# Stick-breaking prompt attention: the sums of the later key blocks are built up on VectorE instead of in TensorE's accumulation

## What is computed

```python
def sb_weights(z, valid):
    log_stay = jnp.where(valid, jax.nn.log_sigmoid(-z), 0.0)
    log_after = lax.cumsum(log_stay, axis=z.ndim - 1, reverse=True) - log_stay
    return jnp.where(valid, jnp.exp(jax.nn.log_sigmoid(z) + log_after), 0.0)

def sb_attend(qb, qpos, k, v, kpos, bias):
    z = sb_logits(qb, k, bias)
    a = sb_weights(z, kpos[None, :] < qpos[:, None])
    return jnp.einsum('bhqk,bkhd->bqhd', a.astype(v.dtype), v)
```

## Time and profile before

| what | value |
|---|---|
| median of three runs | 1826.12 us (1821.38 to 1830.33) |
| the profiled execution | 1838.87 us, its span 1837.0 us |
| TensorE busy | 1698.0 us, 92% of the span |
| VectorE busy | 701.4 us, 38% |
| ScalarE busy | 441.0 us, 24% |
| GpSimd busy | 186.4 us, 10% |
| mean granted TensorE clock | 0.936 of full speed |

### The profile page before, as it was taken

The page is one execution under the profiler, slowest core; times in us unless marked ns, Lnnn a source line. Parts: engine busy times, 40 slices in busy tenths (PEclk is TensorE's granted clock), DMA queues, the critical chain, the costliest instruction groups (busy, mean ns, idle before and its releaser), DMA issues.

```text
span 1837.0 us, 27196 instructions
## 1 busy us (share of the span) xinstructions
PE 1698.0 (92%) x10382; PEld 1443.8 (79%) x10382; DVE 701.4 (38%) x2932; ACT 441.0 (24%) x648; POOL 186.4 (10%) x271
## 2 busy tenths in 40 slices
PE   6997978879999779999899799999998999999997
PEld 4886856657777368998797577777887999999996
DVE  2048547656888435344502200000234323332223
ACT  2001145422232422222301220000124222222112
POOL 1000001100000055355103100000000000000000
PEclk9998988979999789999769899999988999999998
DMA  3269644447887100000054778773421323332231
GB/s 96 69 228 315 226 176 133 128 161 270 275 285 273 38 1 1 1 1 1 13 172 138 229 240 275 239 261 119 117 59 57 92 82 91 93 90 77 85 94 47
DMA packets 222895, 245.73 MB, mean 134 GB/s; under 512 B 8985, under 2 KB 184211, under 8 KB 222723
## 3 DMA queue, kind: packets, MB, share of 16 engines
q1 hardware_dynamic: 222766, 244.00, 41.6%
HBM read 232.56 MB, written 11.60 MB: 133 GB/s over the span
## 4 chain that ended last, share of the span: by engine, by line
PE 83%; DVE 6%; DMA 4%; ACT 3%; POOL 2%; issue 1%; SPq 1%; POOLq 0%; DVEq 0%; ACTq 0%
PE ps L713 32%; PE ps L731 24%; PE ps L757 3%; PE ps L808 3%; PE ps L955 3%; DMA kring<-in_cache_k 2%; PE ps L966 2%; PE ps L821 2%; PE ps L970 2%; PE ps L698 1%; PE ps L1041 1%; DVE kring L1469 1%; PE ps L855 1%; PE ps L781 1%; POOL kring L1977 1%
## 5 line engine op out<-in xcount | busy, mean ns | idle before, releaser
L713 PE MATMUL ps<-xn,wring 128*128 128x268 f32 (+1 forms) x2336 | 544.5, 394 | 7.0 <-DVE xn L1452 4.4
L713 PEld LDWEIGHTS ps<-xn,wring 128*128 128x128 f32 (+1 forms) x2336 | 442.2, 191 | 116.4 <-issue 29.4
L1469 DVE CUSTOM_DVE_ANT_0 kring<-kring,qv 128x128 f32<-128x128 f32 x1024 | 225.0, 289 | 74.3 <-DMA kring<-in_cache_k 74.1
L1168 ACT ACTIVATE R<-ps 128x536 f32<-128x536 f32 x86 | 53.0, 616 | 511.7 <-PE ps L713 349.8
L426 DVE TENSOR_TENSOR wring_split<-wring,vring_split 128x1024 fp32r<-128x1024 f32 (+1 forms) x76 | 90.8, 1195 | 212.0 <-ACT vring_split L419 212.0
L731 PE MATMUL ps<-xn_split,vring_split 128*128 128x268 f32 x704 | 146.3, 289 | 8.0 <-DVE obT_split L440 8.0
L731 PE MATMUL ps<-obT_split,vring_split 128*128 128x268 f32 x704 | 145.1, 288 | 0.0
L731 PE MATMUL ps<-xn_split,wring_split 128*128 128x268 f32 x704 | 144.7, 287 | 0.0
L419 ACT ACTIVATE vring_split<-wring 128x1024 fp32r<-128x1024 f32 (+1 forms) x76 | 78.5, 1034 | 178.7 <-DMA wring<-in_w_ffn_out 106.8
L731 PEld LDWEIGHTS ps<-xn_split,vring_split 128*128 128x128 f32 x704 | 110.6, 190 | 8.8 <-issue 7.8
L731 PE MATMUL ps<-R_split,vring_split 128*128 128x268 f32 x592 | 114.1, 290 | 2.3 <-DVE rows_split L440 2.3
(11 more groups left out here) (333 smaller groups left out, 2159.6 us busy)
## 6 DMA issues: line engine op xcount, KB each, us to landing
kring<-in_cache_k SPq DMA_DIRECT2D x128, 512.0 KB, 5.0
vring<-in_cache_v SPq DMA_DIRECT2D x76, 512.0 KB, 5.4
wring<-in_w_in SPq DMA_DIRECT2D x72, 512.0 KB, 4.6
kring<-in_cache_v SPq DMA_DIRECT2D x52, 512.0 KB, 4.9
wring<-in_w_ffn_in SPq DMA_DIRECT2D x44, 512.0 KB, 3.8
wring<-in_w_ffn_out SPq DMA_DIRECT2D x16, 512.0 KB, 3.7
qv<-qdram SPq DMA_DIRECT2D x8, 512.0 KB, 6.1
out_rec_sample<-R SPq DMA_DIRECT2D x4, 1024.0 KB, 9.1
```

Of the source, the lines that this page charges most:

```text
L713: last = mm(ps[0:m, 2 * (t % 2) + i, 0:HALF], w_block(p, kk), src[:, k, i * HALF:i * HALF + HALF], start=(k == 0), stop=(k == n_k - 1))
L1168: go(halves(dst), pair(t, m), func).then_inc(act_read, 1)
L1469: m = v.tensor_tensor_reduce(kh, kh, qbc[:, b % 2, h * P:h * P + P], 1.0, 0.0, ALU.mult, ALU.add, dz[:, b % 4, p * H + h:p * H + h + 1])
```

## The change

One more triangle, tri_lt (ones where the key is above the diagonal, the complement of tri_ge), is made with the constants. VectorE gets a function suffixes: after GpSimd has masked sps of a head, it adds the rows of block kt + 1 to those of block kt, from the last block to the first, so that block kt then holds, partition by partition, its own softplus values and those of all later blocks. The five additions of a head wait for each other by a semaphore, s_suf. TensorE's later_sums then takes at most two matmuls per piece: tri_ge times block kt, and tri_lt times block kt + 1 (since tri_ge + tri_lt is the matrix of ones, this is the same sum). TensorE waits for s_suf in place of s_msp.

```diff
-CONSTS = 11
+CONSTS = 12
...
+SUFFIX = [(3, 512, LP), (2, 384, LP), (1, 256, LP), (0, 128, 512), (0, 512, LP)]
+
...
                 def later_sums(h):
-                    pe.wait_ge(s_msp, h + 1)
+                    pe.wait_ge(s_suf, len(SUFFIX) * (h + 1))
                     if h >= 1:
                         pe.wait_ge(s_arg, h)
                     for kt, a, b, bank, col in SB_PIECES:
-                        parts = [(tri_ge, kt, a)] + [(ones, k2, max(a, P * k2)) for k2 in range(kt + 1, TT)
-                                                     if P * k2 < b]
+                        parts = [(tri_ge, kt, a)]
+                        if kt + 1 < TT and P * (kt + 1) < b:
+                            parts.append((tri_lt, kt + 1, max(a, P * (kt + 1))))
...
+                def suffixes(h):
+
+                    dve.wait_ge(s_msp, h + 1)
+                    for i, (kt, a, b) in enumerate(SUFFIX):
+                        f, f2 = sb_at(kt, a)[2], sb_at(kt + 1, a)[2]
+                        if i:
+                            dve.wait_ge(s_suf, len(SUFFIX) * h + i)
+                        v.tensor_tensor(sps[:, h % 2, f:f + b - a], sps[:, h % 2, f:f + b - a],
+                                        sps[:, h % 2, f2:f2 + b - a], ALU.add).then_inc(s_suf, 1)
+
                 for h in (0, 1):
                     magnitude(h)
                     softplus(h)
+                suffixes(0)
+                suffixes(1)
                 for h in range(H):
                     dve.wait_ge(s_c, h + 1)
...
                     if h + 2 < H:
                         softplus(h + 2)
+                        suffixes(h + 2)
...
-            for m in (ones, tri_ge, tri_le, tri_gt):
+            for m in (ones, tri_ge, tri_le, tri_gt, tri_lt):
...
+            keep(tri_lt[:, :], tri_lt[:, :], [[1, P]], 0, -1, ALU.is_gt).then_inc(const_ready, 1)
```

More of the change, by code:

```diff
@@ L230, in build @@
         tri_gt = sb("tri_gt", [P, P])
+        tri_lt = sb("tri_lt", [P, P])
         lvl, lvl2 = twins("lvl", [P, 7, P])
@@ L373, in build @@
         s_s, s_z, s_abs, s_exp, s_ln, s_sp = (sem(n) for n in ("s_s", "s_z", "s_abs", "s_exp", "s_ln", "s_sp"))
+        s_suf = sem("s_suf")
         s_msp, s_c, s_arg, s_marg, s_w, s_av, s_o = (sem(n) for n in ("s_msp", "s_c", "s_arg", "s_marg", "s_w", "s_av", "s_o"))
@@ L1886, in _ @@
             g_.memset(selv[:, :], 0.0).then_inc(const_step, 1)
-            pool.wait_ge(const_step, 7)
+            pool.wait_ge(const_step, 8)
             keep(ident[:, :], ident[:, :], [[-1, P]], 0, 1, ALU.not_equal, 1.0).then_inc(const_ready, 1)
@@ L1898, in _ @@
                 keep(v[:, :, 0, :], v[:, :, 0, :], [[-2 * s, nb], [0, s]], -s, 1).then_inc(const_step, 1)
-            pool.wait_ge(const_step, 7 + 14)
+            pool.wait_ge(const_step, 8 + 14)
             for i in range(7):
```

## The result

The changed kernel takes 1833.26 us, the median of seven runs (1828.89 to 1836.76). Before takes 1822.82 us, the median of seven runs (1821.38 to 1830.33). The medians are 10.4 us apart and the means of the seven 8.5. The ratio, taken from all runs of both, is 1.0046, with a 95% interval of 1.0026 to 1.0067: slower by some 8 us, where 1.9 us less had been forecast. Measured once more beside other kernels, the ratio was 1.0031 (1.0013 to 1.0048), some 6 us.

A forecast was written before the change was run, and what follows sets the result against it. The prediction took TensorE, 83% of the chain, as the bound, with later_sums on each attention round's path. It summed +4.8 (start) - 4.8 (six rounds) - 1.9 (seventh) = -1.9 us: 1837.0 profiled, 1824.2 median, range 1816 to 1836.

The forecast's parts named there:

- The two paths of a round: Attention round: TensorE's path falls from 16.62 to 14.7 us, the VectorE and GpSimd path with additions grows to 16.64.
- later_sums is 1.9 us shorter: TensorE, each head: 8 of 19 matmuls go, which saves 1.91 us, taken as 1.9.
- So the round stays as it is: 16.64 against 16.62.: Attention round: VectorE's additions end 16.61 us behind args, so next args starts at 16.64 against 16.62 before.
- 4.8 us lost: Start of attention: later_sums(0) waits for suffixes(0) behind softplus(1), so args(0) starts at 280.6 instead of 275.80.
- 4.8 us gained: Six rounds from args(0) to args(6): 99.8 us instead of 104.59, TensorE's room taking in most low-clock time.
- TensorE's room: Six rounds: TensorE's path has 1.9 us of room in each, which can take in most of a low-clock stretch.
- gets its 1.9 us: Seventh round, args(6) to args(7), 17.47 us before: no softplus or suffixes behind it, so TensorE's saving counts fully.
- TensorE goes on with weight tiles that nothing else delays, so what the stage gains passes on.: Behind the attention stage, which ended at 409 before: the stage's gain reaches the kernel's total time.
- Rival 1: TensorE's clock falls behind pauses of about 4 us: +12.4 us, median 1838.5; chance 0.12 in full, 0.09 half.
- rival 2: VectorE's path has unseen room, so TensorE's 14.7 us sets the round: -13.5 us, median 1812.6; chance 0.07.

The follow-up runs named there:

- after_fill: The changed kernel plus five TensorE matmuls of 384 columns on constants between scores and values, output unread; 1828.69 us, ratio to before 0.9994.
- before_fill: The kernel before plus three TensorE matmuls of 384 columns on constants between scores and values, output unread; 1811.52 us, ratio to before 0.9913.

## Why the prediction was wrong

It was wrong in its sign: -1.9 us forecast, some +6 to +8 measured. The time lies in the range given and the change within the 0.5% that I had taken for no change, but that is the width of the range and not the forecast: the intervals exclude both no difference and a gain. The two paths of a round and what the change does to each were right. Three terms of the sum were not, and all three because of TensorE's clock.

- *"later_sums is 1.9 us shorter."* Measured 4.59 against 6.61 us at full clock, 2.02. Right.
- *"So the round stays as it is: 16.64 against 16.62."* The changed round is 16.55 us, in 16 of the 18 rounds of three profiles. It is on VectorE's path, as after_fill shows. Right for the changed kernel. For the kernel before, the 16.62 was a round at low clock in part; its own full-clock round is 14.95 us, since the 5.21 us of its values are 3.54 at full clock.
- *"4.8 us lost"* at the start. args(0) is 28.4 us behind the first scores in the mean of three profiles, against 24.1 in the mean of four: 4.2 us. Right within 0.6.
- **The step that failed first**: *"4.8 us gained"* in the six rounds. I took 104.59 us for before's length of them. It was the longest of four executions, and their mean is 100.9. The changed kernel's mean is 100.9 as well (99.29, 101.66, 101.66). The gain is nothing. Between the two profiles first shown the rounds did fall by 5.3 us (104.59 to 99.29); that this meets the forecast is chance of the execution that was read. A mean says more here than a row: before's rounds trade between 14.95 and 19.9 us by TensorE's clock, and a pace set by VectorE gives up the short ones together with the long ones. I had written that the low stretches would be hidden by TensorE's room, and not that the short rounds would be lost.
- **The second**: the seventh round *"gets its 1.9 us"*. Round seven and the rest of the stage took 28.4 us before (mean of four) and 28.0 after (mean of three): 0.4 us. The round itself got 1.4 of the 1.9: 17.06 us in the mean before, 15.66 after (17.44 in the profile where values(6) ran wholly at low clock, 14.77 in the two others). Behind args(7) 1.0 was lost again, since values(7) took 6.69 us in all three profiles, wholly at low clock, where before it took 5.49 to 5.88. In after_fill round seven and the rest are 23.6 us.
- **The third**: *"TensorE goes on with weight tiles that nothing else delays, so what the stage gains passes on."* What it loses passes on too, and a little more: up to the first v_quad the loss grows from 3.8 to 5.1 us. Behind values(7) at low clock, the first weight tile took 9.86, 10.07 and 10.07 us after, against 7.46, 9.15, 9.15 and 9.15 in the four profiles of before.

With the measured terms the sum is +4.2 + 0.0 - 0.4 + 1.3 = +5.1 us, against 5.7 us in the second comparison and 8.4 in the first, with intervals that reach down to 2.4 and 4.7 us. The 7.0 us between this and the forecast are -0.6 at the start, +4.8 in the six rounds, +1.5 in the seventh and behind it, and +1.3 behind the stage. What is left over, up to 3 us, I can't place: behind the first v_quad the four profiles of before alone lie between 1397 and 1413 us. It stays open.

Rival 1 said what would make the change slower, but put it into the wrong kernel in part. The low clock of the rounds was already there before, at pauses of 2.03 us. In the change the pauses are 3.96 us, as it had said, in the rounds behind a values of 5.2 us; behind a longer values they are as short as 3.15, behind one of 3.54 us 5.65. The low clock behind them made TensorE's path the longer one (18.93 us) in one round of each of two profiles of three; in the other rounds the room of that path hid it. A round near rival 2's 14.7 us comes once the additions are moved, though it is VectorE's path that then sets half of them.

The Trainium skill's rule on the clock (TensorE: Matmul & The Clock Gate, HAM oscillation) agrees with the filled pauses: where less of the pauses is left, the granted clock is 0.98 and not 0.82 to 0.90. Its shorter price for an addition (VectorE: DVE Perf Modes, the TRN2 errata: 58 cycles) doesn't agree, the section's measured formula does: 384 columns took 0.557 us in the mean, and the formula, (384 + 151) / 0.96 GHz, gives 0.557 as well.

## What to carry to other kernels

Work that is taken from one engine and put on another has a place in the second engine's order, and the place can cost more than the work: five additions of 1.79 us in all took back the whole gain of some 13 us ahead of an instruction that somebody waits for, and behind it no more than the ratios can tell. Before a duration that contains matmuls enters a sum, look whether its rounds are all at the same granted clock, and take several executions; where they vary, a pace set by another engine loses the short ones as well. Where TensorE pauses once a round for a chain on other engines, a few matmuls on constants in the pause may be worth trying first: here they gave more (0.9913) than the change they were meant to explain took away.

## What was not expected of the hardware

A pause of 2.03 us in a round of 15 us is enough to bring the granted clock down in most rounds: 18 of before's 24 rounds in four profiles were longer than 14.95 us, and none of six in the one profile with the pause filled. Which rounds it hits differs from execution to execution of the same kernel (the six rounds together between 96.39 and 104.59 us). These 8.2 us are part of the 17.9 us between the longest and the shortest of the four spans. Filling the pauses gave more than the rounds alone explain: before_fill is some 16 us faster than before, of which the six rounds are 11.2, the start 0.5, round seven and what follows it in the stage 0.9, and the way to the first v_quad 1.3. I haven't placed the remaining 2 us.
